# Feature-wise products of a split-precision transformer step: three matmuls of 256 columns into one sum, and results read by ScalarE alone

## What is computed

```python
def ffn(h, w1, w2):
    a = jnp.maximum(h @ w1, 0)
    return (a * a) @ w2

def rec_mixer(h, w_in, cw, cb, ...):
    xr, g = jnp.split(h @ w_in, 2, axis=-1)
    xr = depthwise_conv(xr, cw, cb)
    ...
```

## Time and profile before

| | |
|---|---|
| median of 3 runs | 2437.95 us (2435.16 to 2439.38) |
| the profiled execution: its own time | 2427.85 us |
| its span, first to last instruction | 2426.1 us |
| granted TensorE clock, mean | 0.99 |
| DMA | 593.21 MB, mean 245 GB/s |
| feature sweeps, us from the span's start | ff1_0 496 to 896, rec_in 1307 to 1577, ff1_1 1691 to 2054 |

### The profile page before, as it was taken

The page is one execution under the profiler, slowest core; times in us unless marked ns, Lnnn a source line. Parts: engine busy times, 40 slices in busy tenths (PEclk is TensorE's granted clock), DMA queues, the critical chain, the costliest instruction groups (busy, mean ns, idle before and its releaser), DMA issues.

```text
span 2426.1 us, 30503 instructions
## 1 busy us (share of the span) xinstructions
PE 2341.6 (97%) x12307; PEld 1823.3 (75%) x12307; DVE 1417.5 (58%) x1927; ACT 1054.4 (43%) x1404; POOL 81.9 (3%) x139
## 2 busy tenths in 40 slices
PE   6999999999999999999999999889999999999997
PEld 2766666678877887777777777766888888778886
DVE  3455754565555565565547767876665556556554
ACT  2432343433333344444444357754444444445443
POOL 2000000000000000000000011100000000000000
PEclk9999999999999999999999999999999999999999
DMA  8899997967766757777786967646766665766652
GB/s 307 305 335 333 319 317 272 320 227 259 257 248 245 269 184 264 264 265 259 256 282 217 319 241 266 213 153 212 245 190 182 199 190 183 252 204 225 207 191 105
DMA packets 305469, 593.21 MB, mean 245 GB/s; under 512 B 20368, under 2 KB 20624, under 8 KB 305072
## 3 DMA queue, kind: packets, MB, share of 16 engines
q1 hardware_dynamic: 299376, 576.90, 69.1%
q0 software_dynamic: 5952, 14.36, 1.9%
HBM read 587.76 MB, written 3.42 MB: 244 GB/s over the span
## 4 chain that ended last, share of the span: by engine, by line
PE 86%; DVE 5%; DMA 4%; ACT 2%; issue 1%; SPq 0%; POOL 0%; DVEq 0%; ACTq 0%; POOLq 0%
PE bank L656 22%; PE bank L646 15%; PE bank L647 14%; PE bank L648 14%; PE bank L658 11%; PE bank L603 6%; DVE w_lo L1276 2%; DMA raw<-in_w_ada 2%; PE bank L797 1%; DMA raw<-in_w_rec_in 1%; PE bank L631 1%; ACT w_hi L974 1%; DMA raw<-in_w_att_in 1%; DMA bias_rows<-in_b_ada 1%; PE bank L673 1%
## 5 line engine op out<-in xcount | busy, mean ns | idle before, releaser
L1276 DVE TENSOR_TENSOR w_lo<-raw,w_hi 128x1024 fp32r<-128x1024 f32 x712 | 861.3, 1222 | 506.4 <-ACT w_hi L974 500.6
L974 ACT ACTIVATE w_hi<-raw 128x1024 fp32r<-128x1024 f32 x712 | 744.0, 1055 | 771.2 <-PE bank L658 275.2
L656 PE MATMUL bank<-xt,w_hi 128*128 128x512 f32 x2560 | 910.1, 400 | 11.0 <-DVE w_lo L1276 8.8
L658 PE MATMUL bank<-xt,w_lo 128*128 128x256 f32 x2560 | 714.5, 279 | 0.0
L646 PE MATMUL bank<-w_hi,xt 128*128 128x512 f32 x1568 | 623.6, 398 | 17.4 <-DVE w_lo L1276 15.5
L647 PE MATMUL bank<-w_lo,xt 128*128 128x512 f32 x1568 | 612.0, 390 | 0.0
L648 PE MATMUL bank<-w_hi,xt 128*128 128x512 f32 x1568 | 611.8, 390 | 0.0
L656 PEld LDWEIGHTS bank<-xt,w_hi 128*128 128x128 f32 x2560 | 482.5, 188 | 160.5 <-issue 31.0
L658 PEld LDWEIGHTS bank<-xt,w_lo 128*128 128x128 f32 x2560 | 483.7, 189 | 0.4
L646 PEld LDWEIGHTS bank<-w_hi,xt 128*128 128x128 f32 x1568 | 294.9, 188 | 147.2 <-issue 55.9
L648 PEld LDWEIGHTS bank<-w_hi,xt 128*128 128x128 f32 x1568 | 295.0, 188 | 63.6
(11 more groups left out here) (186 smaller groups left out, 910.3 us busy)
## 6 DMA issues: line engine op xcount, KB each, us to landing
raw<-in_w_ff SPq DMA_DIRECT2D x512, 512.0 KB, 4.7
raw<-in_w_ada SPq DMA_DIRECT2D x384, 512.0 KB, 7.1
raw<-in_w_att_in SPq DMA_DIRECT2D x72, 512.0 KB, 5.4
raw<-in_w_rec_in SPq DMA_DIRECT2D x64, 512.0 KB, 6.5
raw<-in_w_att_out SPq DMA_DIRECT2D x32, 512.0 KB, 5.6
raw<-in_w_rec_out SPq DMA_DIRECT2D x32, 512.0 KB, 4.2
gain_rows<-in_g_post_mix POOLq DMA_DIRECT2D x8, 256.0 KB, 5.5
gain_rows<-in_g_post_ffn POOLq DMA_DIRECT2D x8, 256.0 KB, 5.2
```

The costliest lines, as they stand in the source:

```text
L656: nc.tensor.matmul(ps[m][:, :], w_hi[:, h, k, m * P:(m + 1) * P], xt[:, c, :], start=(begin and k == 0), stop=False)
L658: mm = nc.tensor.matmul(ps[m][:, 0:NG * T], w_lo[:, h, k, m * P:(m + 1) * P], xt[:, c, 0:NG * T], start=False, stop=(end and k == 1))
L974: nc.scalar.activation(w_hi[:, n % NSPLIT, :, :], raw[:, T4.p % NRAW, 2 * q:2 * q + 2, :], ACT.Copy)\
L1276: V.tensor_tensor(w_lo[:, n % NSPLIT, :, :], raw[:, T4.p % NRAW, 2 * q:2 * q + 2, :], w_hi[:, n % NSPLIT, :, :].bitcast(fp32), ALU.subtrac ...
```

## The change

In `feature_half` the matmul of 512 columns and the one of 256 become three of 256, all into columns 0 to 255 of the bank: hi x hi, the same weights again against the lo columns, and lo x hi. There is then one sum and nothing in columns 256 to 511. ScalarE alone reads a result: a copy with Relu for the MLP, a plain copy otherwise, with `chunk_read`. After the fourth result of an MLP block it waits for its own four copies and squares them in place, 128x1024, with one step of `hidden_ready` for the block in place of four. VectorE's `feature_out` (L1310 and L1313) goes, and so does `lo_copied`; the wait in ScalarE's `split` and `hidden0` count blocks.

```diff
                 for k in range(2):
                     c = (2 * hh + k) % KC
-                    nc.tensor.matmul(ps[m][:, :], w_hi[:, h, k, m * P:(m + 1) * P], xt[:, c, :],
-                                     start=(begin and k == 0), stop=False)
-                    mm = nc.tensor.matmul(ps[m][:, 0:NG * T], w_lo[:, h, k, m * P:(m + 1) * P],
-                                          xt[:, c, 0:NG * T], start=False, stop=(end and k == 1))
+                    o, x_hi, x_lo = ps[m][:, 0:NG * T], xt[:, c, 0:NG * T], xt[:, c, NG * T:2 * NG * T]
+                    hi, lo = (w[:, h, k, m * P:(m + 1) * P] for w in (w_hi, w_lo))
+                    nc.tensor.matmul(o, hi, x_hi, start=(begin and k == 0), stop=False)
+                    nc.tensor.matmul(o, hi, x_lo, start=False, stop=False)
+                    mm = nc.tensor.matmul(o, lo, x_hi, start=False, stop=(end and k == 1))
...
                 if T4.s.tiles == 16:
                     if T4.blk == 0:
-                        act.wait_ge(hidden_ready, hidden0[T4.s.name] + 2 * h + 2)
+                        act.wait_ge(hidden_ready, hidden0[T4.s.name] + h // 2 + 1)
...
-                at = 4 * (s.col0 + T4.blk) + m
                 if s.out == "xr":
-                    dst = gel[:, m:m + 1, :]
+                    dst = gel[:, m, :]
                     if m == 0 and T4.blk > 0:
                         act.wait_ge(conv_ready, 4 * T4.blk)
                 else:
-                    dst = hidden[:, at:at + 1, :]
-                nc.scalar.activation(dst, ps[m][:, NG * T:2 * NG * T].rearrange("p (o t) -> p o t", o=1), ACT.Copy)\
-                    .then_inc(lo_copied, 1)
+                    dst = hidden[:, 4 * (s.col0 + T4.blk) + m, :]
+                nc.scalar.activation(dst, ps[m][:, 0:NG * T], ACT.Relu if s.out == "hidden" else ACT.Copy).then_inc(chunk_read, 1)
+                if s.out == "hidden" and m == 3:
+                    four = hidden[:, 4 * T4.blk:4 * T4.blk + 4, :]
+                    act.wait_ge(chunk_read, 4 * T4.sum + 4)
+                    nc.scalar.activation(four, four, ACT.Square).then_inc(hidden_ready, 1)
...
-            hidden0 = {"ff2_0": 0, "ff2_1": 4 * FF // BLK}
+            hidden0 = {"ff2_0": 0, "ff2_1": FF // BLK}
...
-            def feature_out(T4, m):
-                s, n = T4.s, 4 * T4.sum + m
-                dve.wait_ge(lo_copied, n + 1)
-                if s.out == "xr":
-                    dst = gel[:, m, :]
-                else:
-                    dst = hidden[:, 4 * (s.col0 + T4.blk) + m, :]
-                V.tensor_tensor(dst, ps[m][:, 0:NG * T], dst, ALU.add).then_inc(chunk_read, 1)
-                if s.out == "hidden":
-                    dve.wait_ge(chunk_read, n + 1)
-                    V.scalar_tensor_tensor(out=dst, in0=dst, scalar=0.0, in1=dst, op0=ALU.max, op1=ALU.mult)\
-                        .then_inc(hidden_ready, 1)
-
```

More of the change, by code:

```diff
@@ L275, in hybrid_step @@
         out_read_dve = sem("out_read_dve")
-        lo_copied = sem("lo_copied")
         chunk_read = sem("chunk_read")
@@ L1322, in out @@
                         token_out(T4, g)
-                else:
-                    for m in range(4):
-                        feature_out(T4, m)
             def ada_sum_out(b):
```

## The result

The changed kernel takes 2452.47 us (median of 4 runs, 2449.76 to 2456.13) against 2437.69 us (4 runs): +14.8 us, ratio 1.0062 (95% interval 1.0044 to 1.0081). It is slower, as forecast, and by about half of the forecast +28. The two profiled executions stand further apart than the medians: spans of 2447.9 and 2426.1 us, +21.8.

What follows compares the result with a forecast made beforehand. TensorE, busy 97% of the span, was taken to bound the kernel; 26.0 us (both MLPs) + 3.6 (recurrent product) - 2 (VectorE relief) = +27.6, say +28, on the median 2437.95 gave 2466 us, range 2434 to 2481.

Steps and rivals of the forecast that it cites:

- +28: Whole kernel: the forecast slowdown in us, rounded from 26.0 + 3.6 - 2 = +27.6.
- rival 1: TensorE: the short slot is free, three of 115.5 ns, only VectorE's relief remains; 2436 us, chance 0.13.
- the slot: TensorE: a 256-column matmul with its load takes 119.7 ns, so a triple takes 359.1 against 346.4 ns, +12.7.
- the base of the median: Whole kernel: +28 was put on the median 2437.95 us, 10.1 us above the profiled execution's 2427.85.
- Rivals 1 and 2: TensorE: short slot free, 2436 us (0.13); or cost by columns, slot half of 226.7 ns, 2420 us (0.08).
- ff1_1 +13.0 us: Second MLP's first product: 1024 triples at +12.7 ns each, all on the chain of waits, 13.0 us.
- ff1_0 +13.0 us: First MLP's first product: 1024 triples at +12.7 ns each, all on the chain of waits, +13.0 us.
- the matmul term (+3.6 us): Recurrent input product: +12.7 ns for the 61% and 51% of pairs on the chain; bounds 0 and 6.5 us.
- The relief of VectorE: Recurrent input product: -2 us from dropping VectorE's L1310 and its adds; bounds 0 and -8; nothing in the MLPs.
- The wait for L1310: Recurrent input product: TensorE's 1.8 us of waiting for this VectorE line should be gone.
- ScalarE, refills, table loads, instruction fetches at 0: MLP blocks: new square covered by 1.4 us of slack; later refills, Relu and Square tables, 5120 more instructions cost nothing.
- Rival 3: TensorE: the weight load becomes the bound and adds to 12.7 ns; slot 135, triple 405, 2573 us; chance 0.05.

Runs made afterwards that it cites:

- e10: Kernel before with the first matmul of a chunk 384 columns wide instead of 512, in ff1_1 alone; ff1_1 311.7 us, 292.9 ns a pair, no whole time given.
- e8: Kernel before with each chunk's 256-column matmul ahead of the 512-column one, except in a block's first chunk; 2428.63 us, ratio 0.9973.
- e6: Kernel before with the change (three matmuls, ScalarE reads alone) in the recurrent input product only, both MLPs as before; 2434.80 us, ratio 0.9997.
- e2: Changed kernel with the 512 and 256 pair back in place of the triple, ScalarE alone reading; 2432.29 us, ratio 0.9995 to the kernel before.
- b2: Kernel before, unchanged, profiled a third time; that execution took 2434.67 us.
- e3: Kernel before with the three 256-column matmuls, still read by both engines (ScalarE's copy multiplied by 0); 2457.18 us, ratio 1.0091.
- e5: Changed kernel with the third matmul of a chunk split into two of 128 columns, in ff1_1 alone; 2559.00 us, one execution.

## Why the prediction was right, and where its size was off

The direction and the mechanism were right: one more matmul with its load has its price, and the chains of both MLPs carry it in full. The time of 2452.5 us lies in the range, but the range was wide, 2434 to 2481, and took in rival 1 with nothing paid at all; the slot in the trace is what separates the two. Of the 13 us by which +28 was too much, the base of the median is some 7, the recurrent product 3.8 and ff1_0 2.8.

- **The slot** (119.7 ns, +12.7 a triple): right. 120.0 in the trace, and e10 bears out the fixed part at another width. Reading it from sums over stretches paid off, where single starts offered 115.5. Rivals 1 and 2 fall. So does the rule of N/2.4 + 2.5 ns, which the page gives for the gap of an isolated matmul (the Trainium skill, "TensorE: Matmul & The Clock Gate", "Back-to-back issue gap"): the trace doesn't agree, 120.0 ns stand against its 109.
- **ff1_1 +13.0 us**: right against the first profile, +13.1.
- **ff1_0 +13.0 us**: measured +10.2. The step that failed is the base of 346.4 ns, taken from one clean stretch of ff1_1 and used for every pair. In the first profile ff1_0 has stretches in the slow rhythm (622.13 us above), where a triple costs 6 to 7 ns more than the pairs and not 13. They hold 409 of the 1024 pairs, and 409 x 6.7 ns is 2.7 us, nearly all of the 2.8 that are missing.
- **The base of the median**: this is the larger part. The prediction put a difference found from the profiled execution on a median 10.1 us above it and asked only how far apart they stand, not why. Two of three profiles of before have ff1_1 7 us longer. Against those the change costs 6.0 to 6.4 us there (375.5 less 369.5 or 369.1), and the stages sum to +6 + 10.2 - 2.2 = +14, against +14.8 and +17.9 measured. That the unprofiled runs of before mostly have the slow rhythm fits the medians, e8 and the gap of 7 us between e6's fastest run and its other eleven, but it can't be seen in them and isn't shown.
- **The recurrent product**: the matmul term (+3.6 us) was right with ScalarE's readout: 3.3 from e2 to the changed kernel. The relief of VectorE was the mis-sized term by this way of taking the change apart: -2 taken, -5.5 measured in e2's profile against the first of before (-4.4 against b2's 267.9 us), inside the bounds of 0 to -8. By the other way, over e3, the matmuls cost 0.3 and the readout gives 2.5, so that the first term would be the wrong one; the runs show the sum, -2.2 against +1.6, and don't settle how it divides. The chain in the earlier trace rows has VectorE for a fifth to a quarter of this stage; the prediction had counted only what TensorE's waits named. That the chain is the reason is argued and not shown, and e10's 265.4 us for the old code here says how far one execution can be trusted. The wait for L1310 is gone, as forecast.
- **ScalarE, refills, table loads, instruction fetches at 0**: right, as far as the traces show: no wait of TensorE is new in the MLPs.
- **Rival 3** named the right resource and the wrong law: the load is a floor of 112 to 116 ns, which 120 clears, and isn't added to the fixed part. Where the Trainium skill says that loads overlap matmuls only in another row group ("TensorE: Matmul & The Clock Gate", Part 3, "The mechanism"), the trace doesn't agree: a 256-wide slot with its load takes 120.0 ns. Another sentence of the same section also lets a load run ahead into the background weight buffer, which the prediction left out; that one the trace doesn't contradict.

## What to carry to other kernels

In these runs a matmul of this precision costs its columns plus 13 ns, and never less than its weight load of 112 to 116 ns, so equal work in more matmuls costs time even when no column is added: 1024 more of them in one stage were 13 us, or 6 where the pairs before ran in their slow rhythm. Take such prices from counts over long stretches. Before adding a difference to a median, ask why the profiled execution stands off it: two more profiles of the kernel before showed 7 us of the answer. And an engine that is relieved counts where it is on the chain of waits, not only where another engine's wait names it.

## What the runs showed of the hardware

- The same pairs of matmuls (512 and 256 columns) run in two rhythms, 345.9 and 352.6 ns on average over 220 us, at full granted clock and without a wait, in different executions of one program. A rhythm holds until TensorE is interrupted, by another matmul or a pause, and can change only there; in ff1_1 it held for 320 us. With the 256-wide one first, ff1_1 took 363.3 to 363.7 us in all three profiles (635 pairs in 220 us), near the fast rhythm. What chooses the rhythm stays open: no run set it on purpose.
- Three equal slots of 256 columns show no second rhythm in any of the four profiles of triples read (611, 611, 612 and 612 in 220 us).
- The time of a matmul with its load of 128x128: 112 ns at 2 columns, 463.2 / 4 = 115.8 on average in e5's mix, 120.0 at 256 columns, 172.9 at 384 (292.9 less 120.0), 226.7 at 512.
- The floor of the load follows the clock: the 2-column matmuls of L631 start 112 ns apart with a clock of 1.00 (26.40 to 27.20 us in the trace of before) and 213 ns apart with 0.50 (39.10 to 39.90 us).
